# Query and key norms and latent products merged into one stage by chunks of tokens, with roots computed once per chunk on stacked rows

## What is computed

```python
def mixer_features(h, w_in, a_q_norm, a_k_norm, b_q_norm, w_q_up, b_kv_norm, w_kv_up, lb, rope_a, rope_b):
    aq, ak, av, bqd, bkvd, bkr, ... = jnp.split(h @ w_in, SPLIT_AT, axis=-1)
    aq = rms_norm(aq.reshape(bsz, t, A_HEADS, HEAD_DIM), a_q_norm)      # 8 heads of 64
    ak = rms_norm(ak.reshape(bsz, t, A_KV_HEADS, HEAD_DIM), a_k_norm)   # 2 heads of 64
    bq = (rms_norm(bqd, b_q_norm) @ w_q_up).reshape(bsz, t, B_HEADS, B_NOPE + B_ROPE)     # rank 192
    bkv = (rms_norm(bkvd, b_kv_norm) @ w_kv_up).reshape(bsz, t, B_HEADS, B_NOPE + B_V)    # rank 128
    if rope_a is not None:            # latent tokens; context tokens are not turned
        aq, ak = apply_rope(aq, rope_a), apply_rope(ak, rope_a)
        bq_pe, bk_pe = apply_rope(bq_pe, rope_b), apply_rope(bk_pe, rope_b)
```

## Time and profile before

| | us |
|---|---|
| median of 3 runs | 4123.89 (4119.31 to 4123.97) |
| the profiled execution, its own time | 4126.54 |
| its span, first to last instruction | 4124.4 |
| PE busy in the span | 3498.6 (85%) |
| DVE busy | 2177.1 (53%) |
| ACT busy | 1234.8 (30%) |
| POOL busy | 801.4 (19%) |
| mean granted PE clock | 0.907 of 2.4 GHz |

### The profile page before, as it was taken

The page is one execution under the profiler, slowest core; times in us unless marked ns, Lnnn a source line. Parts: engine busy times, 40 slices in busy tenths (PEclk is TensorE's granted clock), DMA queues, the critical chain, the costliest instruction groups (busy, mean ns, idle before and its releaser), DMA issues. The chain is left out here.

```text
span 4124.4 us, 46083 instructions
## 1 busy us (share of the span) xinstructions
PE 3498.6 (85%) x18861; PEld 1749.4 (42%) x18861; DVE 2177.1 (53%) x3575; ACT 1234.8 (30%) x1725; POOL 801.4 (19%) x412
## 2 busy tenths in 40 slices
PE   4898456679999999999998798455799899999997
PEld 2555342222234555555554544332222265444444
DVE  4681888656644533333335782877666445333334
ACT  2221335324434411111113332244244343112212
POOL 0000641038770000000000000621188600000000
PEclk8898678679999999999999898677699999999999
DMA  5210004210003011111110210032100031111111
GB/s 193 62 35 0 1 1 176 100 39 10 1 11 118 10 42 42 41 41 41 42 36 21 82 41 5 1 112 83 33 9 1 26 92 37 51 51 52 50 53 41
DMA packets 215156, 194.22 MB, mean 47 GB/s; under 512 B 10215, under 2 KB 180002, under 8 KB 214434
## 3 DMA queue, kind: packets, MB, share of 16 engines
q1 hardware_dynamic: 210786, 182.89, 14.4%
q10 hardware_dynamic: 4160, 8.39, 0.6%
HBM read 167.48 MB, written 14.68 MB: 44 GB/s over the span
## 5 line engine op out<-in xcount | busy, mean ns | idle before, releaser
L719 PE MATMUL feed_acc<-feed_aa,feed_w 128*128 128x512 f16 (+1 forms) x3936 | 761.6, 355 | 0.0
L719 PE MATMUL feed_acc<-hh,feed_w 128*128 128x512 f16 (+1 forms) x3936 | 753.8, 354 | 5.2 <-DVE feed_w L1001 5.2
L719 PEld LDWEIGHTS feed_acc<-feed_aa,feed_w 128*128 128x128 f16 x3936 | 387.5, 98 | 376.3 <-issue 14.8
L719 PEld LDWEIGHTS feed_acc<-hh,feed_w 128*128 128x128 f16 x3936 | 386.0, 98 | 370.1 <-DVE feed_w L1001 5.8
L1942 POOL TENSOR_TENSOR at_accp<-at_accp,at_p 128x1024 f32<-128x1024 f32 x192 | 451.4, 2351 | 82.7 <-ACT at_p L1975 74.2
L355 PE MATMUL in_acc<-hh,in_w 128*128 128x512 f16 (+1 forms) x2088 | 400.7, 355 | 65.0 <-DVE in_w L345 52.5
L1996 DVE TENSOR_REDUCE at_mx<-at_small 128x1 f32<-128x512 f32 (+1 forms) x492 | 316.9, 686 | 256.2 <-PE at_small L2052 253.6
L1975 ACT ACTIVATE at_p<-at_sT 128x1024 f32<-128x1024 f32 x246 | 252.1, 1025 | 365.7 <-PE at_sT L2081 365.7
L355 PEld LDWEIGHTS in_acc<-hh,in_w 128*128 128x128 f16 (+1 forms) x2088 | 208.3, 100 | 255.5 <-DVE in_w L345 53.3
L1060 DVE SCALAR_TENSOR_TENSOR y<-feed_acc,y 128x1280 f32<-128x1280 f32 (+1 forms) x96 | 130.3, 1357 | 331.5 <-PE feed_acc L719 331.5
L1047 DVE TENSOR_TENSOR feed_r<-feed_r 128x1280 f32<-128x1280 f32 (+1 forms) x56 | 76.1, 1359 | 418.9 <-ACT feed_r L854 418.9
(11 more groups left out here) (281 smaller groups left out, 4455.0 us busy)
## 6 DMA issues: line engine op xcount, KB each, us to landing
pre<-in_w_ff SPq DMA_DIRECT2D x84, 512.0 KB, 4.0
pa_wada<-in_w_ada SPq DMA_DIRECT2D x16, 2048.0 KB, 11.0
feed_stage<-in_w_ff SPq DMA_DIRECT2D x44, 512.0 KB, 4.0
in_stage<-in_w_in SPq DMA_DIRECT2D x36, 512.0 KB, 4.2
set_wada<-in_w_ada ACTq DMA_DIRECT2D x4, 2048.0 KB, 21.5
pb_wada<-in_w_ada SPq DMA_DIRECT2D x4, 2048.0 KB, 9.5
pre<-in_w_out SPq DMA_DIRECT2D x12, 512.0 KB, 4.9
x<-x_scratch SPq DMA_DIRECT2D x3, 2048.0 KB, 9.3
```

Source lines behind the costliest of these rows:

```text
L719: last = nc.tensor.matmul(out[:, b:b + cn], w[:, wh, k, m0:m0 + P], src[:, sh, k, a + b:a + b + cn], start=(k == 0 and wh == 0 and sh == 0 ...
```

## The change

`prepare_norms` and `prepare_latent` become one stage, `prepare`, whose items go chunk by chunk: rotary key, the flat tiles, the rotary tiles, keys, values, latent queries (21 items in a latent chunk, 19 or 9 in the context's).

- The sums of squares of a chunk's eight tiles are collected by eight matmuls of 32 columns (four column groups) in 12 rows of one PSUM bank, already divided. One mean, one Ln and Exp and one Newton step follow for a chunk. A matmul with a 0/1 matrix (`cast`) spreads a tile's rows over its partitions again, into PSUM, where DVE reads the factor.
- The gains go into two copies of the cosine table, into the rotation matrices (`spin`), and into DVE's product of the flat tiles; ACT's pass with the gain and POOL's cosine product are gone (DVE multiplies by the cosine). Context tokens are no longer turned.
- The next chunk's squares (ACT), sums (PE) and mean and Newton step (DVE) stand among this chunk's items.
- Rings of four in `u`; five PSUM banks in a ring for roots, rotations and products. The rotary key's low half is written for one head by DVE and copied to three by ACT (`spread`).
- All adaLN pieces (12 in layer 0, 8 in layer 1) are in this stage, one turn every five items, ring of two.
- Tables and weights are loaded at the stage's start, into `hh` and `bv`, which are free then.
- The unused parameter `ahead` of `between` is removed.

```diff
+SUMS = [("ak", 0, 0), ("bkv", 1, 32), ("aq0", 2, 64), ("aq1", 3, 96), ("aq2", 4, 0), ("aq3", 5, 32), ("bq0", 6, 64),
+        ("bq1", 7, 64)]
...
+def prepare(nc, e, sem, l, f):
...
+    for c, (a, n) in enumerate(cks):
+        lat, query = a < LAT, a < nq
+        start.append(len(items))
+        items.append(("kpe" if lat else "kraw", 0, c))
+        items.append(("flat", "bkv", c))
+        if query:
+            items += [("flat", "bq0", c), ("flat", "bq1", c)]
+        names = ["ak"] + (["aq0", "aq1", "aq2", "aq3"] if query else [])
+        items += [("rope" if lat else "flat", x, c) for x in names]
+        items += [("bk", h, c) for h in range(4)]
+        items += [("bv", t, c) for t in range(a // P, (a + n) // P)]
+        if query:
+            items += [("bq" if lat else "bqraw", h, c) for h in range(4)]
...
+        turn_at = {2 + 5 * j: j for j in range(ada.n)}
...
+                for q in range(4):
+                    square(0, q)
+                evacuate(0)
+                act.wait_ge(s_ca, 32)
+                nc.scalar.activation(cos["ak"], cos["aq"], ACT.Copy, scale=e.sv[:, l, R_AK:R_AK + 1]).then_inc(s_cos, 1)
...
+                root(0)
+                for i in range(N + 1):
+                    if i + 1 < N:
+                        evacuate(i + 1)
+                    if i:
+                        high(i - 1)
...
+                    if at == 4:
+                        spread(c)
+                    if c + 1 < len(cks):
+                        if 0 <= at - 6 < len(pieces(c + 1)):
+                            square(c + 1, at - 6)
+                        if at == 17:
+                            root(c + 1)
...
+                def add(c, q):
...
+                    return nc.tensor.matmul(S[g:g + 32, 0:n], sums[0:R, j, :], sq[0:R, q % 4, 0:n],
+                                            start=(q == same[0]), stop=(q == same[-1]), tile_position=(0, g))
...
+                        if kind == "rope":
+                            free(i, "rot")
...
+                            nc.tensor.matmul(bank(i, "rot")[:, 0:n], spin[:, int(h == "ak"), :], operand[h][:, a:a + n],
+                                             start=True, stop=True)
+                        free(i, "root")
+                        pe.wait_ge(s_n, c + 1)
...
+                        nc.tensor.matmul(bank(i, "root")[0:D0, 0:n], cast[0:R, j, 0:D0], rs[0:R, c % 2, 0:n],
+                                         start=True, stop=True).then_inc(s_p, 1)
...
+                for i in range(N + 1):
+                    if i < N:
+                        main(i)
+                    if i:
+                        rotate(i - 1)
...
+                    if c + 1 < len(cks):
+                        if at == 10:
+                            four(c + 1, 0)
+                        if at == 15 and len(pieces(c + 1)) > 4:
+                            four(c + 1, 4)
+                    if i in turn_at:
+                        if turn_at[i]:
+                            ada.cols(pe, turn_at[i] - 1)
+                        ada.rows(pe, turn_at[i])
...
+                    if kind == "rope":
+                        dve.wait_ge(s_p, outs[i] + 1)
+                        ch(nc.vector.tensor_tensor(t1[:, 0:n], bank(i, "rot")[:, 0:n], sin[:, a:a + n], ALU.mult))
+                        ch.wait(dve)
+                        ch(nc.vector.tensor_tensor(u[:, i % 4, 0:n], u[:, i % 4, 0:n], t1[:, 0:n], ALU.add))
+                        ch.wait(dve)
+                        nc.vector.tensor_tensor(u[:, i % 4, 0:n], u[:, i % 4, 0:n], bank(i, "root")[:, 0:n], ALU.mult)\
+                          .then_inc(s_u, 1)
...
+                for i in range(N + 2):
+                    if i < N:
+                        turn(i)
+                    if i >= 2:
+                        low(i - 2)
+                    if i >= N:
+                        continue
+                    finish(i)
...
+                        if at == 17:
+                            mean(c + 1)
+                        if at == 18:
+                            refine(c + 1)
```

More of the change, by code:

```diff
@@ L86, in __init__ @@
         self.s_pad = sem(nm + "cact_padded")
-        self.n = last - first
+        self.n = len(groups)
     def pad(self, dve):
@@ L162, in setup_phase @@
         ce = sb("ce", [P, 2 * KT])
[L163 removed]
+        A = Ada(nc, e, sem, st, "set_", [(0, j) for j in range(4)], 4)
         lbw = sb("lbw", [P, 6, 4])
@@ L1165, in _ @@
             def _(sp):
-                for j in range(ada.n if ada else 0):
-                    ada.load(sp, j)
                 if store:
@@ L1602, in _, with free @@
             def _(pe):
-                pe.wait_ge(s_ul, 3)
+                passes = ((0, 0), (0, 1), (1, 0))
+                def free(i, role):
+                    j = slot[i, role] - 5
+                    if j < 0:
+                        return
+                    i0, was = uses[j]
+                    if was == "up" and items[i0][0] == "bq":
+                        pe.wait_ge(s_first, firsts[i0] + 1)
+                    elif was == "up":
+                        pe.wait_ge(s_lo, i0 + 1)
+                    else:
+                        pe.wait_ge(s_u, dones[i0] + 1)
@@ new lines, in add @@
+                def add(c, q):
+                    name, j, g = pieces(c)[q]
+                    n = cks[c][1]
+                    same = [k for k, x in enumerate(pieces(c)) if x[2] == g]
+                    pe.wait_ge(s_sq, sum(len(pieces(b)) for b in range(c)) + q + 1)
+                    if c and q < 4:
+                        pe.wait_ge(s_m, c)
+                    R = operand[name].shape[0]
+                    return nc.tensor.matmul(S[g:g + 32, 0:n], sums[0:R, j, :], sq[0:R, q % 4, 0:n],
+                                            start=(q == same[0]), stop=(q == same[-1]), tile_position=(0, g))
@@ L1605, in rotate, with four @@
+                def four(c, q0):
+                    for q in range(q0, min(q0 + 4, len(pieces(c)))):
+                        last = add(c, q)
+                    last.then_inc(s_sum, 1)
                 def rotate(i):
-                    kind, h, a, n = items[i]
+                    kind, h, c = items[i]
                     if kind in rows:
+                        n = cks[c][1]
                         lo, hi_ = rows[kind]
-                        pe.wait_ge(s_xg, rots[i] + 1)
-                        nc.tensor.matmul(prot[i % 3][lo:hi_, 0:n], e.swap[lo:hi_, 1, lo:hi_], xg[lo:hi_, i % 3, 0:n],
-                                         start=True, stop=True).then_inc(s_p2, 1)
@@ L1613, in _ @@
[L1613 to L1617 removed]
+                        free(i, "rot")
+                        pe.wait_ge(s_first, firsts[i] + 1)
+                        nc.tensor.matmul(bank(i, "rot")[lo:hi_, 0:n], e.swap[lo:hi_, 1, lo:hi_], u[lo:hi_, i % 4, 0:n],
+                                         start=True, stop=True).then_inc(s_rot, 1)
```

562 lines of the change are left out of this document (264 added, 298 removed).

## The result

| | before | after |
|---|---|---|
| median of 4 runs | 4122.03 us (4119.31 to 4123.97) | 4020.91 us (4017.19 to 4023.08) |
| ratio, 95% interval | | 0.9754 (0.9737 to 0.9771) |
| profiled execution, span | 4124.4 us | 4017.8 us |
| layer 0, norms and latent products | 218.9 us | 156.4 us |
| layer 1, the same | 183.0 us | 136.1 us |

Faster by 101 us; the forecast was 4045 us, range 4002 to 4092. Stages run here from the clearing of `cpad` (VectorE) to the clearing of `at_ks` (GpSimd), as in all that follows. They lost 109.4 us together; the rest of the program took 2.8 us longer, so the gain is not elsewhere.

What follows compares the result with a forecast made beforehand. VectorE was taken to bound the norms, while no engine filled the latent products. Head, two chunks, context and end gave 171.6 us (-47.4) in layer 0 and 151.6 (-31.9) in layer 1: -79 us, 4045 us, range 4002 to 4092.

Steps and rivals of the forecast that it cites:

- Removed work, 94 us at most: VectorE work taken out of both layers' stages, about 56 and 38 us, if all was on the path.
- The factor from PSUM at no surcharge: Root products read their factor from PSUM at the same price as from SBUF, 684 against 688 ns.
- Head 19 and 5: Stage start: root ready near 19 us, then 5 us for the key's rotation on cold PE and what follows.
- (a): Chunk section with key rotation, three flat and five rotary tiles: 23.5 us warm, 38 cold.
- (b): Chunk section from last rotary tile to first latent query's rotation, PE's queue exposed, a new wait: 16 us warm, 28 cold.
- (c): Chunk section of four latent queries plus the next chunk's mean and root: 13.5 us warm, 16 cold.
- A chunk 59.3 us, by mixing 53 and 82 at a clock of 0.85: One 512-token latent chunk: 53 us at full clock, 82 at half, with 30% of the time at half.
- Context and end, 29 us in layer 0, 9 in layer 1: Context chunk, then last turn and finishes: 24 and 5 us in layer 0, 7.5 and 1.5 in layer 1.
- A: Rival: PE's clock holds at full speed in the merged stage, -114 us, 4010 us; chance 0.20.
- B: Rival: merged stage runs as loosely as the latent stages, VectorE 58% busy, 4063 us; chance 0.21.
- C: Rival: PE becomes the bound, its clock at half through both stages, +32 us, 4156 us; chance 0.05.
- D: Rival: the removed work was hidden and the time stays; chance 0.02.

Runs made afterwards that it cites:

- the order that was the most even on paper: Latent queries also placed between the rotary tiles, against the interleaved kernel with the early rotary key (3981.3 us): 4035.8 us.
- the context's part alone: Kernel before the change, with only the turning of context tokens removed: 4115.1 us against 4119.1.

## Why the prediction was right, and what was mis-sized

- *Removed work, 94 us at most.* Measured 96 us, and put back it cost 92 us and more: right. It was no bound on the whole change, though: the gain in the stages, 109 us, passed it, and by the run that put the work back 7 to 11 us belong to the rest of the change. The sum itself left out the seven narrow L1481 of layer 0, stretched to 693 ns, some 2 us.
- *The factor from PSUM at no surcharge.* 686 ns for L1680 against 693 for L1678: right for the rotary tiles. The flat tiles' product L1688 takes 748 ns. By the figure of the Trainium skill ("VectorE: DVE Perf Modes", the section on the TRN2 errata) the 42 products would have cost an estimated 2.7 us more. L1680 disagrees with it, as the rows before did; in L1688 factor and gain came together, and L1720, with an operand in PSUM and a constant, takes 683 ns.
- *Head 19 and 5.* First root at 642.5, 18.6 us after the stage's start, and 4.0 us of waiting behind it: right. The early rotary key shortened that wait to 2.2 us: VectorE's first root product came 21.4 us into the stage and not 24.7.
- *Sections at full clock, 23.5, 16, 13.5.* (a) took 24.3 us where PE has room (the run with no turn beside it) and 24.4 to 25.7 in the changed kernel; at full clock (b) took 15.6 and (c) 13.9. Right, and (b) was PE's queue with VectorE waiting 7.6 us at its end, the forecast's new wait. Its two parts stand as forecast: the late squares say when the queue starts (PE waits for them 4.6 us in layer 0), PE's own work how long it is, as the run with the turns moved shows.
- *A chunk 59.3 us, by mixing 53 and 82 at a clock of 0.85.* **This step failed.** The clock was right (0.83, 0.82), the mixing was not: chunks took 54.8, 57.0, 56.2 and 48.2 us, together 216 and not 237, 21 us less. Done section by section, the same mixing gives 26.5, 18.4 and 14.2 us, and over the four chunks (a) was some 6 us shorter than that, (b) 12 and (c) 2. In (a) half clock was charged though VectorE sets the length there: 24.3 us at 0.84 to 0.89 with no turn beside it. In (b) 9 of the 12 us are the last chunk of layer 1, 9.8 us for 18.4, priced like the others though it has two sums for the next chunk and no late square to wait for. The other three (b), at clocks of 1.00, 0.77 and 0.90, make up the remaining 4 us.
- *Context and end, 29 us in layer 0, 9 in layer 1.* 21.8 and 9.2: 7 us too dear in layer 0, where the clock was 0.97 and the four turns had been priced between warm and cold.
- *Rivals.* The time, 4021 us, is nearer to A's 4010 than to the forecast's 4045, and the stages are nearly A's (153 and 135.5 us, against 156.4 and 136.1), but not by A's mechanism: the clock did not hold. B fell with VectorE 63% and 68% busy; its 95 us of new work in layer 1 did not follow from its rows either (129.1 - 38 = 91, measured 92.0), and with 91 it would have stood near 4056. C fell with the doubled root spread, D with the work put back.

Repaired, the step reads: 24.5 and 14 us for (a) and (c), with a microsecond more where a turn at half clock falls into (a); (b) by the clock of that section, 15.6 to 18.3 us as measured; and 10 us for (b) where the next chunk has no query tiles.

## What to carry to other kernels

Price each section of a stage by the engine that fills it, and let a resource's slowness (here the granted clock) count only in the sections that wait for that resource. Once one engine's work has been thinned, look for stretches in which two engines take turns being full: moving side work (adaLN turns) or light items across them gave another 22 to 23 us each, for a table of numbers or a loop. Evenness has its limit: the order that was the most even on paper cost 48 us, with the leading engine waiting for banks and a lower clock. And check a gain against the busy time that it is said to save: moving the cosine product saved VectorE nothing, though the time came out where it was expected.

## What the runs showed of the hardware

- GpSimd's product holds VectorE up by operands, not by presence. Beside GpSimd's fp32 product, an instruction with one operand in PSUM kept its 0.69 us (L1680 at 655.08), one with two in SBUF took 1.15 (L1683 at 655.80), and one that began 0.02 us after GpSimd's 1.80 us, 0.52 more than GpSimd's own 1.28 (L1729 at 657.57). The Trainium skill ("SBUF — State Buffer", section "SBUF: two separate sides") describes the shared pair of ports as an exclusive lock that such an instruction and GpSimd's hold for the whole instruction, whoever starts first. The three rows agree with it.
- 42 added matmuls cost nothing in sum: the clock of layer 0's stage was 0.91 and not 0.83, the stages' sum +0.4 us. The clock moves with other edits too (0.87 with the cosine product on GpSimd and no matmul added), so that the matmuls raised it is not shown.
- A copy of 128x16 values on VectorE, both ends in SBUF, beside GpSimd's clearing of `kb` lasts 3.96 us, and 0.18 in the first norms of the kernel run for the context's part alone, where nothing stands beside it. Timeline of VectorE, then of GpSimd, kernel after:

```profile
624.22 3.96 DVE L93 COPY pre_cpad<-cact 128x16 f32<-128x16 f32 x1
```
```profile
623.79 4.36 POOL L1424 MEMSET kb<- 1x5120 f16 x1 [51.95 <-POOLq L2481]
```

  It ends within 0.03 us of the clearing, as the lock would have it, and is covered by the loads at the head of both layers.
- The flat tiles' product (L1688, the factor in PSUM and a gain per partition from SBUF) lasts 748 ns, some 60 more than products with a constant (L1720, one operand in PSUM, 683) or without a third operand (L1680, 686).
